# A hybrid decoder step: the key transposes of a retention head move behind a value unit and the probability transposes

## The reference

```
for one retention head, chunks of 128 tokens:
    q, k = rotary(q), rotary(k) * dk ** -0.5
    att  = (q @ k.T) * dmat                       # dmat: causal decay
    o    = att @ v + (q @ S) * q_decay
    S    = chunk_decay * S + (k * k_decay).T @ v
```

## Time and profile before

| | us |
|---|---|
| median of 3 runs | 1072.98 |
| lowest, highest | 1071.91, 1078.2 |
| the profiled execution | 1073.26 |
| its span | 1071.4 |
| PE busy | 999.7 (93%) |
| PEld busy | 926.7 (86%) |
| DVE busy | 539.9 (50%) |
| ACT busy | 380.3 (35%) |
| POOL busy | 151.2 (14%) |

### The profile page before, as it was taken

The page is one execution under the profiler, slowest core; times in us unless marked ns, Lnnn a source line. Parts: engine busy times, 40 slices in busy tenths (PEclk is TensorE's granted clock), DMA queues, the critical chain, the costliest instruction groups (busy, mean ns, idle before and its releaser), DMA issues.

```text
span 1071.4 us, 21575 instructions
## 1 busy us (share of the span) xinstructions
PE 999.7 (93%) x7796; PEld 926.7 (86%) x7796; DVE 539.9 (50%) x1017; ACT 380.3 (35%) x605; POOL 151.2 (14%) x149
## 2 busy tenths in 40 slices
PE   5999999999999999999989989999988999999892
PEld 5999999999999999778877777878757999999892
DVE  4246335433633454566656755675675433224338
ACT  4035213422431344345425442633454334333100
POOL 0001010101101012232312231322210000000003
PEclk8999999999999999999999999999988999999997
DMA  8775674767556564365638454643680888776602
GB/s 284 247 258 192 229 255 168 255 234 260 184 198 208 206 229 168 130 227 207 203 109 277 154 184 141 243 167 130 207 281 20 281 286 297 256 264 232 216 21 88
DMA packets 137317, 219.51 MB, mean 205 GB/s; under 512 B 7936, under 2 KB 102784, under 8 KB 135552
## 3 DMA queue, kind: packets, MB, share of 16 engines
q1 hardware_dynamic: 132704, 205.77, 56.5%
q0 software_dynamic: 3920, 10.89, 3.0%
q10 hardware_dynamic: 656, 2.36, 0.6%
HBM read 206.40 MB, written 99.88 MB: 286 GB/s over the span
## 4 chain that ended last, share of the span: by engine, by line
PE 84%; DVE 9%; ACT 3%; issue 2%; DMA 1%; DVEq 0%; ACTq 0%; SPq 0%; POOL 0%; POOLq 0%
PE bank L685 18%; PE bank L687 18%; PE bank L686 18%; PE bank L680 8%; PE bank L715 4%; PE bank L958 4%; PE bank L919 3%; DVE part_l L1574 3%; PE bank L772 2%; PE bank L794 2%; PE bank L994 1%; PE bank L1003 1%; PE bank L936 1%; ACT part_h L1256 1%; DMA xn<-in_x_prompt_dram 1%
## 5 line engine op out<-in xcount | busy, mean ns | idle before, releaser
L685 PE MATMUL bank<-xh,wh 128*128 128x288 f32 x640 | 193.1, 302 | 0.4 <-PE bank L1091 0.4
L685 PE MATMUL bank<-wh,xh 128*128 128x256 f32 x640 | 188.1, 294 | 3.5 <-DVE wl L1368 3.0
L687 PE MATMUL bank<-xh,wl 128*128 128x288 f32 x640 | 189.3, 296 | 0.0
L686 PE MATMUL bank<-xl,wh 128*128 128x288 f32 x640 | 189.2, 296 | 0.0
L686 PE MATMUL bank<-wl,xh 128*128 128x256 f32 x640 | 183.2, 286 | 0.0
L687 PE MATMUL bank<-wh,xl 128*128 128x256 f32 x640 | 183.1, 286 | 0.0
L685 PEld LDWEIGHTS bank<-wh,xh 128*128 128x128 f32 x640 | 125.3, 196 | 6.3 <-issue 3.4
L1132 ACT ACTIVATE wh<-raw 128x1024 fp32r<-128x1024 f32 (+1 forms) x104 | 101.2, 1018 | 80.1 <-PE bank L715 69.8
L686 PEld LDWEIGHTS bank<-wl,xh 128*128 128x128 f32 x640 | 125.2, 196 | 1.4
L687 PEld LDWEIGHTS bank<-wh,xl 128*128 128x128 f32 x640 | 124.8, 195 | 0.0
L685 PEld LDWEIGHTS bank<-xh,wh 128*128 128x128 f32 x640 | 121.0, 189 | 1.7 <-issue 1.4
(11 more groups left out here) (208 smaller groups left out, 1844.6 us busy)
## 6 DMA issues: line engine op xcount, KB each, us to landing
cslot<-in_cache_kv_w_dram SPq DMA_DIRECT2D x48, 1024.0 KB, 5.9
out_dram<-in_cache_kv_w_dram SPq DMA_DIRECT2D x20, 2040.0 KB, 10.4
raw<-in_w_in_dram SPq DMA_DIRECT2D x128, 256.0 KB
out_dram<-in_cache_kv_w_dram SPq DMA_DIRECT2D x24, 1020.0 KB, 9.5
out_dram<-in_cache_kv_w_dram SPq DMA_DIRECT2D x20, 504.0 KB, 5.2
raw<-in_w_in_dram SPq DMA_DIRECT2D x16, 512.0 KB
out_dram<-in_cache_kv_w_dram SPq DMA_DIRECT2D x24, 252.0 KB, 3.2
out_dram<-kv POOLq DMA_DIRECT2D x16, 256.0 KB, 3.3
```

Of the source, the lines that this page charges most:

```text
L685: pe.matmul(out, lhs[0](k), rhs[0](k), start=(k == 0), stop=False)
L686: pe.matmul(out, lhs[0](k), rhs[1](k), start=False, stop=False)
L687: last = pe.matmul(out, lhs[1](k), rhs[0](k), start=False, stop=(k == n - 1))
```

## The change

In `retention_head` of PE's list, the four transposes of the rotated keys (`group(3)`) stood between `sample_att` and `value_unit(2)`. They now stand behind `value_unit(2)` and `cached_probs(0)`, directly in front of `sample_output`. The lists of the other engines are the same.

```diff
                 blocks(lambda t, c: turn(b[:, c], rot[:, t, 0:RK]))
                 value_unit(1)
                 sample_att()
+                value_unit(2)
+                cached_probs(0)
                 b = group(3)
                 blocks(lambda t, c: turn(b[:, c], rot[:, t, RK:2 * RK]))
-                value_unit(2)
-                cached_probs(0)
                 sample_output()
                 for n in range(4):
                     sample_state_group(n)
```

## The result

| | before | the change |
|---|---|---|
| median, us (18 runs each) | 1074.74 | 1081.24 |
| lowest, highest | 1071.91, 1078.5 | 1075.83, 1084.25 |
| the profiled execution | 1073.26 | 1083.47 |
| its span | 1071.4 | 1081.5 |
| mean granted clock over that span | 0.974 | 0.965 |

The ratio is 1.0043, with a 95% interval of 1.0026 to 1.0059: the change makes the kernel slower by 0.4%, about 4.6 us, where 0.84 was forecast, and 1.6 as the far end of that term. The range ended at 1079.0; the median, 1081.24, lies above it. The sum of the forecast started from 1073.26, the profiled execution; the median of 18 runs of before is 1074.74, so 1.5 of the 7.1 us between 1074.1 and 1081.24 lie in the base, not in the change. Against the bound of 1% the outcome is "same", which had 0.94.

A forecast was written before the change was run, and what follows sets the result against it. PE's chain of waits was taken to bound the kernel (84%). The profiled 1073.26 us plus 0.84 for a later L992 in four heads, with clock drops unchanged, gave 1074.1 us; range 1071.5 to 1079.

The forecast's parts named there:

- The old wait goes, a new one comes: Key transposes: PE's 2.10 us wait for VectorE goes; before L992 PE waits about two microseconds for GpSimd's `km`.
- The size of the wait: L984 to L992: 6.44 us (6.30 to 6.62) against 6.23, +0.21 a head, +0.84 for four heads.
- The neighbourhood of GpSimd and VectorE: VectorE's remainders beside GpSimd's `km` product: costed at nothing; `km` keeps 1.89 us, or remainders are held, unneeded by PE sooner.
- The rival in which the remainders hold GpSimd: `km` beside L1574: held behind the remainders, +2.10 a head, 1081.7; chance 0.14 without further drops, 0.04 with.
- half-pace case: `km` beside the remainders, each at half the pace: about +1.3 us a head, 1078.5; within the 0.14 for GpSimd held.
- one clock drop in four heads stays one in four: Idle stretch before the sample output: still about two microseconds, so one head in four drops, at 1.53 us.
- The rival of more drops: Behind the idle stretch: three or four heads drop the clock, +3.1 to +4.6 us, 1077.2 to 1078.7; chance 0.16.

The follow-up runs named there:

- the control: The kernel of before with its order for PE, only `km` moved into the place of `schain`; ratio to before 0.9995 (0.9981 to 1.001).
- wait then unit 3: The change with value unit 3 taken from the cached output to ahead of the sample output, PE waiting for `km` before that unit; ratio to before 1.0046.
- output behind the old wait: Before with `km` in the place of `schain` and the sample output moved directly behind the key transposes, ahead of value unit 2; ratio to before 1.0267.

## Why the prediction was wrong

**The old wait goes, a new one comes.** Right, and where it was said: the transposes wait for nobody, PE idles in front of L992 with L620 as the releaser, 2.33 us in the third head. The run with `km` in its own place shows that this wait alone, and not the order, keeps the move from gaining: 0.99 instead of 1.004.

**The size of the wait.** L992 at 6.64 and not 6.44, since the release took 0.35 us (L620 ends at 649.94, L992 starts at 650.29). I had taken 0.20 between 0.06 and 0.38; it was the long end, plus 0.05 for the transposes' start. +0.4 a head instead of +0.21 in the first three, +0.3 in the fourth, 1.5 us instead of 0.84 in all. The single head lies 0.02 beyond the far end of 6.62, the sum within its 1.6.

**The neighbourhood of GpSimd and VectorE.** Right in both parts. `km` kept its 1.89 us, the three remainders took 3.06 instead of 1.89, and nobody missed them. VectorE still waited for L994 before its copy, 6.04 us in the third head and 2.83 in the second, where the clock stayed up:

```profile
556.41 0.42 DVE L1678 COPY rot<-bank 64x256 f32<-64x256 f32 x1 [2.83 <-PE bank L994]
```

The rival in which the remainders hold GpSimd didn't happen. Its half-pace case was summed wrongly: the 1.32 us more count from L992 at 6.44, not from 6.23, so it is +1.5 a head and 1079.4, not +1.3 and 1078.5, and lay just outside the range that was said to take it in. By the Trainium skill, "SBUF — State Buffer", section "Who interferes with whom", the second to issue of such a pair is held until the first is through; the trace agrees: the first remainder starts 0.57 behind `km`, takes 1.86 us instead of 0.69 and ends 0.55 behind it, and the three end at 651.68, 1.17 us late.

**The step that failed** is "one clock drop in four heads stays one in four", with its price of 1.53 us. It was mis-sized twice. The price was read from a drop that had a dense value unit behind it, and carried over to a place where the sample output stands behind; I saw that L994 is bound by its matmuls and would run at half pace, and took it for granted that the drop would last no longer than the 3.4 us seen. In five of the six drops in the two traces of the change it lasted 6.8 us, most of the sample output, and cost 3.0 to 3.2 us; in the sixth it lasted 3.4 and cost 1.7. And the count was read from one execution: it was three of four in both traces of the change, and the control shows three of four for before's own list of PE too, so one of four was no count to carry over. By the mean clocks, before spends 51 us at 1.2 GHz and the change 63.
The rival of more drops was the right mechanism, with 0.16 and too low a price. With the measured sizes its sum is 1073.26 + 1.4 - 1.5 + 9.4 = 1082.6, and the profiled execution took 1083.47.

**What stays open.** That a drop can last and cost twice as much with the sample output behind it is shown by the seven traces that have drops: eight of twelve did there, none of eight ahead of a value unit. Why the other four didn't is not shown. Whether drops also come more often there isn't shown either: 12 of 16 heads against 8 of 16, with 0 to 4 of 4 between executions of one row of the table. The key transposes stand ahead of the idle stretch in the change and behind it in before. The other pairings exist too: ahead of it with a unit behind (wait then unit 3) no head dropped, and behind it with the output next (output behind the old wait) three did, two of them long. That points to the output and not to the transposes, but with one execution each. What in the sample output keeps the clock down (the 64 columns of weights, float32 products that the trace lists as two instructions each, or pauses between them) was not tried.

## What to carry to other kernels

Before a producer is moved past work that its consumer hid behind, look for the consumers on other engines that share its memory: here `km` lay in the tile that the moved transposes read, and the version that gives it another place turns +0.4% into -0.9%. When idle time on TensorE is moved but not shortened, don't carry over the price of a clock drop from the old place: here it was 1.5 us ahead of a value unit and up to 3.2 ahead of the sample output, so the price has to be taken from a trace that has the new neighbour. And count drops over several executions, or by the mean clock of all runs: four heads of one trace gave one, and the trace of a kernel with the same order for TensorE three.

## What the runs showed of the hardware

- Filling 2.3 us of idle time with useless matmuls made the kernel 0.56% faster than leaving them out (0.9987 against 1.0043), with 47.2 us at 1.2 GHz on average instead of 62.7.
- A clock drop behind an idle stretch of about two microseconds lasted 3.4 us in eight of eight cases with a value unit behind it (128 columns of weights; in four of them the stretch was in two pieces), and 6.8 us in eight of twelve with the sample output behind it (64 columns).
- A loop body longer by 18 matmuls brought a stall of 5.6 us and one of 4.0 at the loop's branch (5.5 and 0.5 in the other kernel with them), and 42 and 33 packets on the instruction queue instead of 23; 9 added matmuls brought none (0.5, and 23 packets). An experiment that adds instructions should look there first.
- Two idle pieces of 0.86 and 0.87 us with a short group of transposes between them were followed by a drop in all four heads of one execution, as one piece of 2.1 us was in one and in three.
- A VectorE instruction with two operands in SBUF that issued 0.57 us behind GpSimd's was held, 1.86 us instead of 0.69 and 3.06 for the three instead of 1.89, while GpSimd's own 1.89 stayed as it was.
